# A hybrid decoder layer on one core: the first panel of the merge gates moved ahead of the recurrent output projection

## The reference, cut to what matters

```python
h = rmsnorm(x, norm1[l])
z = h @ w_in[l]
...
xr = rg_lru(causal_conv(z_rx, ...), ...)
y_a = (xr * jax.nn.gelu(z_ry)) @ w_rg_out[l]
...
y_b = nsa(q, kc, vc, k_s, kvs(z_vs), k_w, kvs(z_vw), ng) @ w_nsa_out[l]
mg = jax.nn.sigmoid(z_mg).reshape(B, S, 2, D_MODEL)
x = x + (mg[:, :, 0] * y_a + mg[:, :, 1] * y_b) @ w_o[l]
h2 = rmsnorm(x, norm2[l])
x = x + (jax.nn.silu(h2 @ w_gate[l]) * (h2 @ w_up[l])) @ w_down[l]
```

## Time and profile before

| | |
|---|---|
| median of 3 runs | 497.62 us |
| lowest and highest | 497.57, 499.29 us |
| the profiled execution | 500.68 us |
| its span | 499.0 us |
| mean granted TensorE clock | 0.989 |
| PE, DVE, ACT, POOL busy | 486.9, 336.6, 284.9, 15.0 us |
| a weight slot's transfer, issue to landing (median) | 4.8 us |

### The profile page before, as it was taken

One profiled execution on the slowest core, in us unless ns is written; L12 is line 12 of the kernel. 1 busy time (PEld: TensorE's weight loads), 2 busy tenths in 40 slices (PEclk: granted clock), 3 DMA queues, 4 the chain that ended last, 5 costly groups with the idle time before them and its releaser, 6 DMA issues.

```text
span 499.0 us, 7330 instructions
## 1 busy us (share of the span) xinstructions
PE 486.9 (98%) x2848; PEld 420.4 (84%) x2848; DVE 336.6 (67%) x507; ACT 284.9 (57%) x450; POOL 15.0 (3%) x24
## 2 busy tenths in 40 slices
PE   6999999999999989999999999999999999999997
PEld 5998998788998768888887887888888888888885
DVE  3899799788865667657664675866666666654432
ACT  5655886676467786766674443655545554553330
POOL 2000200220000000000000000000000000000000
PEclk9999999999799999999999999999999999999999
DMA  8645767424222453342425462455545554455402
GB/s 312 239 166 214 315 280 276 169 85 169 85 85 85 138 195 104 156 169 85 168 85 175 162 252 86 158 198 210 195 169 174 208 208 169 175 216 199 170 0 84
DMA packets 12688, 84.72 MB, mean 170 GB/s; under 512 B 1520, under 2 KB 1520, under 8 KB 2928
## 3 DMA queue, kind: packets, MB, share of 16 engines
q1 hardware_dynamic: 11952, 82.32, 44.7%
q0 software_dynamic: 272, 1.05, 0.6%
q10 hardware_dynamic: 432, 0.91, 0.5%
HBM read 83.22 MB, written 1.05 MB: 169 GB/s over the span
## 4 chain that ended last, share of the span: by engine, by line
PE 89%; ACT 4%; DVE 3%; DMA 1%; issue 1%; POOLq 0%; POOL 0%; SPq 0%; ACTq 0%; DVEq 0%
PE bank L1060 18%; PE bank L1061 18%; PE bank L1062 18%; PE bank L1100 16%; PE bank L1103 8%; PE bank L1186 2%; PE bank L1197 1%; PE bank L1355 1%; DVE w_lo L656 1%; DMA raw<-stream_dram 1%; ACT pbuf L454 1%; PE bank L1224 1%; ACT w_hi L364 1%; PE bank L1401 1%; DVE ast L765 1%
## 5 line engine op out<-in xcount | busy, mean ns | idle before, releaser
L656 DVE TENSOR_TENSOR w_lo<-raw,w_hi 128x2048 fp32r<-128x2048 f32 x72 | 164.8, 2291 | 72.2 <-ACT w_hi L364 71.7
L364 ACT ACTIVATE w_hi<-raw 128x2048 fp32r<-128x2048 f32 x72 | 137.8, 1915 | 46.0 <-PE bank L1062 45.8
L1100 PE MATMUL bank<-h_hl,w_hi 128*128 128x512 f32 x352 | 89.3, 392 | 0.0
L1100 PEld LDWEIGHTS bank<-h_hl,w_hi 128*128 128x128 f32 x352 | 63.3, 189 | 11.2 <-issue 0.2
L1060 PE MATMUL bank<-w_hi,h_hl 128*128 128x512 f32 x160 | 63.5, 397 | 0.0
L1062 PE MATMUL bank<-w_hi,h_hl 128*128 128x512 f32 x160 | 62.4, 390 | 0.0
L1061 PE MATMUL bank<-w_lo,h_hl 128*128 128x512 f32 x160 | 62.4, 390 | 0.0
L1060 PE MATMUL bank<-w_hi,act 128*128 128x512 f32 x152 | 59.9, 394 | 1.9 <-DVE act L808 1.9
L1061 PE MATMUL bank<-w_lo,act 128*128 128x512 f32 x152 | 59.2, 389 | 0.0
L1062 PE MATMUL bank<-w_hi,act 128*128 128x512 f32 x152 | 59.2, 389 | 0.0
L1103 PEld LDWEIGHTS bank<-h_hl,w_lo 128*128 128x128 f32 x352 | 48.4, 190 | 4.0
(11 more groups left out here) (222 smaller groups left out, 693.0 us busy)
## 6 DMA issues: line engine op xcount, KB each, us to landing
raw<-stream_dram SPq DMA_DIRECT2D x72, 1024.0 KB, 4.8
w<-stream_dram SPq DMA_DIRECT2D x4, 1024.0 KB, 8.7
raw<-stream_dram SPq DMA_DIRECT2D x2, 512.0 KB, 7.4
xs<-x_dram POOLq DMA_DIRECT2D x1, 1024.0 KB, 5.4
out_dram<-xs SPq DMA_DIRECT2D x4, 256.0 KB, 2.0
xs<-x_dram ACTq DMA_DIRECT2D x1, 512.0 KB, 5.2
xs<-x_dram SPq DMA_DIRECT2D x1, 512.0 KB, 5.0
scr<-small_dram ACTq DMA_DIRECT2D x1, 320.0 KB, 8.6
```

The source lines that it names most:

```text
L364: sc.activation(w_hi[:, i % HL, :], raw[:, i % RAW, :], ACT.Copy).then_inc(hi_ready, 1)
L656: ve.tensor_tensor(w_lo[:, i % HL, :], raw[:, i % RAW, :], f(w_hi[:, i % HL, :]), ALU.subtract).then_inc(lo_ready, 1)
L1100: ins = pe.matmul(acc(u + mt)[:, :], w_hi[:, s, c:c + P], a_hl[:, k, :, :].rearrange("p x s -> p (x s)"), start=k == 0, stop=k == KC - 1)
```

## The change

The first panel of the merge gates (two slots, now called `mga`) is put between `ry` and `rgo`; the other three panels (`mgb`, six slots) stay behind `rgo`. So `mga` is slots 20 and 21, `rgo` 22 to 25 and `mgb` 26 to 31. The banks are handed out in the new order. The weights lie in DRAM as before; `IN_STREAM` gives the place of each slot, and SP's loads are written out up to slot 26.

The gelu moves from iterations 19 and 21 to the end of ACT's iterations 20 and 22. y is formed in DVE's iterations 21 and 23, at the same place as before; `y_hi` stands at the end of ACT's iterations 21 and 23, and `y_lo` right behind DVE's `split_lo`. PE waits for y chunk by chunk in the first half of slots 22 and 24. The tanh of the first gate panel comes in ACT's iteration 22, behind the gelu. The gate product of this panel reads the rgo banks directly, in DVE's iteration 25, in place of the copy on ACT and a product in SBUF; the second rgo panel is still copied, in ACT's iteration 26, and multiplied in DVE's iteration 29. The semaphore `m_gated` goes.

```diff
-         ("ry", 4), ("rgo", 4), ("mg", 8), ("nso", 4), ("wo", 4), ("gu", FF), ("dn", FF // 2)]
+         ("ry", 4), ("mga", 2), ("rgo", 4), ("mgb", 6), ("nso", 4), ("wo", 4), ("gu", FF), ("dn", FF // 2)]
...
+IN_STREAM[FIRST["mga"]:FIRST["mgb"]] = [FIRST["rgo"] + 6, FIRST["rgo"] + 7] + list(range(FIRST["mga"] + 4, FIRST["mga"] + 8))
+MG_SLOT = [FIRST["mga"], FIRST["mgb"], FIRST["mgb"] + 2, FIRST["mgb"] + 4]
+MG_USE = [USE["mga"], USE["mgb"], USE["mgb"] + 2, USE["mgb"] + 4]
...
-            for i in range(RAW, 5 * RAW):
+            for i in range(RAW, 9 * RAW):
...
-            with sp.Fori(5, NSLOT // RAW) as rnd:
+            with sp.Fori(9, NSLOT // RAW) as rnd:
...
-                for v in range(2):
-                    if i == FIRST["ry"] + 3 + 2 * v:
-                        u = USE_RY[2 * v + 1]
-                        sc.wait_ge(acc_free[u % 4], u // 4 + 1)
-                        sc.activation(B[:, 4 * v:4 * v + 4, :], B[:, 4 * v:4 * v + 4, :],
-                                      ACT.Gelu_apprx_tanh).then_inc(gelu_ready, 1)
-                for v in range(2):
-                    if i == FIRST["ry"] + 3 + 2 * v:
-                        for n in (2 * v, 2 * v + 1):
-                            sc.wait_ge(y_ready, n + 1)
-                            sc.activation(y_hi[:, 2 * n:2 * n + 2, :], A[:, 2 * n:2 * n + 2, :], ACT.Copy).then_inc(y_hi_ready, 1)
...
+                for v in range(2):
+                    if i == FIRST["ry"] + 4 + 2 * v:
+                        u = USE_RY[2 * v + 1]
+                        sc.wait_ge(acc_free[u % 4], u // 4 + 1)
+                        sc.activation(B[:, 4 * v:4 * v + 4, :], B[:, 4 * v:4 * v + 4, :],
+                                      ACT.Gelu_apprx_tanh).then_inc(gelu_ready, 1)
+                    if i == FIRST["ry"] + 5 + 2 * v:
+                        for n in (2 * v, 2 * v + 1):
+                            sc.wait_ge(y_ready, n + 1)
+                            sc.activation(y_hi[:, 2 * n:2 * n + 2, :], A[:, 2 * n:2 * n + 2, :], ACT.Copy).then_inc(y_hi_ready, 1)
+
+                if i == FIRST["rgo"] + 4:
+                    acc_ready(FIRST["rgo"] + 3)
+                    sc.wait_ge(y_lo_ready, 4)
+                    for t in range(T2):
+                        u = USE["rgo"] + 2 + t
+                        sc.activation(mrg[:, t, 512:1024], acc(u)[:, :], ACT.Copy).then_inc(acc_free[u % 4], 1)
+
+                for pnl in range(4):
+                    if i == MG_SLOT[pnl] + 2:
+                        acc_ready(MG_SLOT[pnl] + 1)
+                        if pnl == 1:
+                            for t in range(T2):
+                                u = USE["rgo"] + t
+                                sc.wait_ge(acc_free[u % 4], u // 4 + 1)
                         for t in range(T2):
-                            u = USE["mg"] + 2 * pnl + t
+                            u = MG_USE[pnl] + t
                             dst = mtt[:, t, :] if pnl < 2 else mt1[:, t, (pnl - 2) * 512:(pnl - 1) * 512]
                             sc.activation(dst, acc(u)[:, :], ACT.Tanh, scale=0.5).then_inc(acc_free[u % 4], 1)
...
                 for v in range(2):
-                    if i == FIRST["ry"] + 3 + 2 * v:
+                    if i == FIRST["ry"] + 5 + 2 * v:
                         for n in (2 * v, 2 * v + 1):
                             ve.wait_ge(gelu_ready, v + 1)
                             ve.tensor_tensor(A[:, 2 * n:2 * n + 2, :], Dr[:, 2 * n:2 * n + 2, :], B[:, 2 * n:2 * n + 2, :],
                                              ALU.mult).then_inc(y_ready, 1)
...
                 if i not in SPLIT_LAST:
                     split_lo(i + AHEAD)
+                for v in range(2):
+                    if i == FIRST["ry"] + 5 + 2 * v:
+                        for n in (2 * v, 2 * v + 1):
+                            ve.wait_ge(y_hi_ready, n + 1)
+                            ve.tensor_tensor(y_lo[:, 2 * n:2 * n + 2, :], A[:, 2 * n:2 * n + 2, :], f(y_hi[:, 2 * n:2 * n + 2, :]),
+                                             ALU.subtract).then_inc(y_lo_ready, 1)
...
+                if i == FIRST["rgo"] + 3:
+                    ve.wait_ge(slot_done, FIRST["rgo"] + 3)
+                    ve.wait_ge(y_lo_ready, 4)
+                    for t in range(T2):
+                        u = MG_USE[0] + t
+                        ve.wait_ge(acc_free[u % 4], u // 4 + 1)
+                        u = USE["rgo"] + t
+                        ve.scalar_tensor_tensor(out=mrg[:, t, 0:512], in0=mtt[:, t, :], scalar=1.0, in1=acc(u)[:, :],
+                                                op0=ALU.add, op1=ALU.mult).then_inc(acc_free[u % 4], 1)
+                if i == MG_SLOT[1] + 3:
...
+                        if chunk_wait is not None and t == 0:
+                            chunk_wait(k)
...
-                        if name == "rgo" and r % 2 == 0:
-                            pe.wait_ge(y_lo_ready, r + 2)
+                        chunk_wait = (lambda k: pe.wait_ge(y_lo_ready, k // 2 + 1)) if name == "rgo" and r % 2 == 0 else None
```

More of the change, by code:

```diff
@@ L51 @@
 ACC_ORDER = [("rx", 4), ("kk", 2), ("rg", 8), ("kc", 1), ("vc", 1), ("qa", 2), ("w1", 1), ("qb", 2),
-             ("vv", 2), ("kcT", 1), ("ry0", 1), ("cmps", 2), ("ry1", 2), ("pcT", 1), ("ry3", 1), ("rgo", 4), ("mg", 8), ("nso", 4), ("wo", 4), ("even", 1), ("gu", 2 * FF), ("dn", 4)]
+             ("vv", 2), ("kcT", 1), ("ry0", 1), ("cmps", 2), ("ry1", 2), ("pcT", 1), ("ry3", 1), ("mga", 2), ("rgo", 4), ("mgb", 6), ("nso", 4), ("wo", 4), ("even", 1), ("gu", 2 * FF), ("dn", 4)]
 USE = {}
@@ L587, in _ @@
                                   ACT.Copy).then_inc(acc_free[u % 4], 1)
[L589 to L593, removed]
-                        for t in range(T2):
-                            u = USE["rgo"] + 2 * pnl + t
-                            sc.activation(mrg[:, t, pnl * 512:(pnl + 1) * 512], acc(u)[:, :], ACT.Copy).then_inc(acc_free[u % 4], 1)
@@ L802, in _ @@
                                              ALU.mult).then_inc(y_ready, 1)
[L804 to L809, removed]
                 if i == HEAD0 + 1:
@@ L967, in _ @@
                         link(ins)
[L969 to L976, removed]
+                if i == FIRST["rgo"] + 3:
[8 more added lines that the diff above has]
+                if i == MG_SLOT[1] + 3:
+                    for t in range(T2):
+                        u = MG_USE[1] + t
+                        ve.wait_ge(acc_free[u % 4], u // 4 + 1)
+                        mv = mrg[:, t, 512:1024]
+                        ve.scalar_tensor_tensor(out=mv, in0=mtt[:, t, :], scalar=1.0, in1=mv, op0=ALU.add,
+                                                op1=ALU.mult)
                 for pnl in range(2):
@@ L1104, in wide, with panel @@
                 ins.then_inc(slot_done, 1)
-            def panel(i, e, u, a_h, a_l, half_done=None, between=None):
+            def panel(i, e, u, a_h, a_l, half_done=None, between=None, chunk_wait=None):
                 slot_ready(i)
@@ L1266, in _ @@
                                compressed_transposed if i == HEAD0 + 2 else None)
-                for name in ("kk", "vv", "qa", "qb", "mg"):
+                for name in ("kk", "vv", "qa", "qb", "mga", "mgb"):
                     r = i - FIRST[name]
@@ L1282, in _ @@
                         between = (lambda: merged_transposed(0)) if (name, r) == ("nso", 3) else None
-                        panel(i, r // 2, USE[name] + r % 2 * 2, *src, wo_half if (name, r) == ("wo", 3) else None, between)
+                        panel(i, r // 2, USE[name] + r % 2 * 2, *src, wo_half if (name, r) == ("wo", 3) else None, between, chunk_wait)
                 r = i - FIRST["rg"]
```

3 lines of the change are left out of this document (1 added, 2 removed).

## The result

| | before | changed |
|---|---|---|
| median | 499.03 us (6 runs) | 502.89 us (6 runs) |
| lowest and highest | 497.57, 499.38 | 501.86, 505.14 |
| the profiled execution | 500.68 | 503.40 |
| its span | 499.0 | 501.7 |

The forecast was 499.8, 2.2 us more than before, with a range up to 501.6: the direction was right, the size about half of what came.

A forecast was written before the change was run, and what follows sets the result against it. PE, busy 98% of the span, was taken as the bound. 3.62 us won against 5.7 to 5.9 lost gave net + 2.2 on the 497.62 median: 499.8 us, range 496.8 to 501.6.

The forecast's parts named there:

- 3.62 us of stalls to win, 1.11 of them in iterations 20 and 21: PE stalls in iterations 20 to 23 cost 3.62 us, all the change can win; removing slot 20's wait gains 1.11.
- The wait returns at slot 22, 2.3 us: Ahead of slot 22, PE waits 2.3 us for y_lo, which now stands behind the 2.21 us split.
- Tanh behind the second gelu pays a table load: ACT, iteration 22: tanh assumed to need a 1.28 us load (lower bound none), making PE lose 1.2 us in iteration 23.
- The wait at slot 24, 0.8 to 2.3 us: Ahead of slot 24, PE idles 0.8 us with a load before tanh, up to 2.3 us without it.
- 0.77 us at slot 26: Slot 26 waits for the bank freed by the gate product: 0.5 us idle plus 0.27 restart.
- Net + 2.2 us: Whole kernel: 3.62 us won against 5.7 to 5.9 lost, so 2.2 us slower.
- rival 3: Stalls at 176, 188 and 197 us bring on the low clock, losing 3.4 us: 503.2 us; chance 0.04.
- the 5.67 us of a slot behind a stall: Time of a panel following a stall, from its first matmul, taken from the trace of before and used for slots 22 and 24.
- The base: Median of the kernel before, 497.62 us, to which the forecast added 2.2 us.
- Rival 1: y is in time at slots 22 and 24 and the stalls vanish: 2.9 us faster, 494.8 us; chance 0.07.
- Rival 4: ACT table switches cost more than their load, 1.35 us dearer each by the skill's rule: 504 us; chance 0.03.

The follow-up runs named there:

- ylo_first: Changed kernel with y_lo put back ahead of split_lo in DVE's iterations 21 and 23; 0.9998 of the kernel before.
- gate_first: Changed kernel with only the first panel's gate product moved ahead of split_lo in DVE's iteration 25; 1.0067 of the kernel before.
- fill: Changed kernel with 15 identity transposes on PE ahead of slots 22 and 24, into a free bank; 1.0040 of the kernel before, 1.0041 when repeated.
- after_again: The changed kernel measured and traced once more, unchanged; 1.0085 of the kernel before, median 503.39 us.
- second_only: Changed kernel with y_lo ahead of split_lo only in iteration 23, still behind it in iteration 21; 1.0033 of the kernel before.
- gelu_mid: Changed kernel with only the second gelu moved into ACT's pause before exp in iteration 22; 1.0036 of the kernel before.
- slots_only: Changed kernel's slot order and gate products, but gelu, y, y_hi and y_lo in their earlier iterations and places; 1.0037 of the kernel before.
- three: Changed kernel with y_lo ahead of split_lo, second gelu in ACT's pause of iteration 22, gate product ahead of iteration 25's split_lo; 0.9942 of the kernel before.
- ylo_gelu: Changed kernel with y_lo ahead of split_lo and the second gelu in ACT's pause of iteration 22, gate product not moved; 0.9966 of the kernel before.

## Why the prediction was wrong

Point by point, by the prediction's own steps.

- **3.62 us of stalls to win, 1.11 of them in iterations 20 and 21.** Right: T(22) - T(20) fell from 17.29 to 16.19.
- **The wait returns at slot 22, 2.3 us.** Right: 2.39, by the chain given (exp held by the load to 171.24 - 167.69 = 3.55 after T(21), measured 3.56). The experiment ylo_first shows that the split ahead of y_lo is the cause.
- **Tanh behind the second gelu pays a table load.** Wrong; of the two bounds I took the wrong one. There was no load, exp paid it, and no wait for o_raw in iteration 23. As worked out, T(25) hardly depends on it (205.0 or 205.2), so this mistake moved the sum by no more than 0.2 us.
- **The wait at slot 24, 0.8 to 2.3 us.** 2.39 measured, the upper bound, which belonged to the case without the load.
- **0.77 us at slot 26.** Right: 0.58 idle with its restart; gate_first gave 0.76 back.
- **Net + 2.2 us.** This sum is near what a kernel at full clock loses. fill, where the chain is untouched and the clock kept, has T(27) - T(20) 2.5 us above before (63.74 - 61.20), and at clock 1.00 takes 2.0 us more than before.
- **The failed step: the low clock behind the new stalls was left out of the sum.** It stood as rival 3, to which I gave 0.04. The reason given against it was that 1.68 us of idle time had been followed by matmuls as fast as ever. That row says nothing about 2.3 us, and my own sum had made two stalls longer than any in the trace of before. The price was about right (3.4; measured 3.1 with both stretches). The measured 4.6 us are the 2.0 to 2.5 of the chain and some 2 to 2.6 of this, since not every execution has both stretches. The term that failed is thus the 5.67 us of a slot behind a stall: taken from a shorter stall, it measured 7.24.
- **The base.** The median of before in three runs, 497.6, was that of a kernel whose executions lie in steps from 497.3 to 501.0; with three more it was 499.0. This is 1.4 us of the 3.1 us between 499.8 and 502.9, and it is chance of which executions came; the other 1.7 are the change itself, 3.9 us between the medians where the sum had 2.2.
- **Rival 1 (faster)** needed y_lo earlier by the 2.21 us of the split. That part is so, but ylo_first shows that it is not enough: the o_raw copy then comes too late by 2.0 us. Three moves together make it true (494.0 to 494.3 us at clock 1.00, against 497.4). **Rival 4** fell with the loads: 1.28 us long, and 1.29 from their start to the next instruction.

What stays open is why one of two equal waits is followed by the low clock and the other isn't. Of eight waits of 2.39 or 2.40 us in five traces (changed, after_again, gate_first, second_only, gelu_mid), five were followed by it. The record narrows this. The three that weren't are all at slot 22, in the three executions whose clock had already been low for a long time near 130 us (0.52, 0.56 and 0.52 over 130 to 137 us in after_again, second_only and gelu_mid). Slot 22 of the changed kernel and of gate_first, where that stretch was shorter (0.82 and 0.81), was followed, and so were the waits of ylo_first and slots_only, whose clock there was 1.00. The mean clocks of all executions fit: the kernels with two waits of 2.4 us (changed, gate_first) had none above 0.993 in 19, those with one (second_only, gelu_mid, slots_only) none above 0.997 in 32, and those with none (before, three, ylo_gelu and both runs of fill) had 0.999 or 1.00 in 48 of 126; ylo_first, with its wait of 1.99 us, had 1.00 in 3 of 12. This is a pattern of a few traces; no run tested it.

## What to carry to other kernels

A change that moves a wait should be summed twice: once at full clock, and once with a stretch at the low clock behind every wait that gets longer than those already seen harmless in the trace. Where a wait can't be taken away, work without use in the gap can keep the clock (here 3.15 us came back for two gaps of 2.4 us); but the cure is to put the short instruction that PE waits for ahead of the long one that it doesn't need yet. And a removed wait uncovers the next: here y_lo, then the o_raw copy, then the gate product, and only the three together paid.

## What the runs showed of the hardware

- Waits of PE of 1.99, 2.39 and 2.44 us were followed by a stretch of about 3.4 us at 1.2 GHz in seven of ten cases; it lengthened the iteration by 1.6 us. Waits of 1.30, 1.34, 1.36, 1.41 and 1.68 us were not followed by one, each seen once; of these 1.34, 1.41 and 1.68 stood in executions with the long low stretch near 130 us. That the kernel before, which has the wait of 1.68 us, reached a mean clock of 1.00 in 34 of 80 executions speaks for that wait being harmless without the long stretch too. Fifteen transposes of the identity in the gap kept the clock in four of four.
- Ahead of this stage, with the same instructions there, some traces have a low stretch near 10 us (0.79 over 8 to 16 us), some near 130 us, some both, as the trace of before, and some neither, as that of three. Of 80 executions of the kernel before, 34 had a mean granted clock of 1.00 (median 497.4 us) and 14 had 0.989 (median 500.8 us): 3.3 us between executions of one kernel. Only one of them was traced, so that the clock is the whole of these 3.3 us is likely but not shown. With differences under 1%, the mean clock of each execution has to be read beside its time.
- Tanh after the tanh-approximated gelu needs no table load (0 us between L584 and L608), as it needs none after exp. A switch costs 1.28 us and no more: in the changed kernel it is 1.29 us from the load's start to exp, and the load ahead of the second gelu (181.15 us) starts 0.02 us after the end of the split before it. The 2.66 us that the Trainium skill (ScalarE: Activation LUTs, What ACT_TABLE_LOAD costs) gives for a switch is not seen in any trace here.
